# Three of eight latent token tiles through all 16384 experts at once, five by gathered expert rows

## What is computed

```python
s = jnp.einsum('thpd,hpnd->thpn', qf, sub_keys)         # 8 heads, 2 halves, 128 keys each
sv, si = lax.top_k(s, 16)
cand = sv[:, :, 0, :, None] + sv[:, :, 1, None, :]       # 256 pairs per head
top_s, pos = lax.top_k(cand, 16)                         # expert = key0 * 128 + key1
gate = softmax(top_s)
act = gelu(einsum('td,thkd->thk', x, u_tab[idx]))        # 128 experts per token
out = einsum('thk,thkd->td', gate * act, v_tab[idx])
```

## Times and profile before

| | us |
|---|---|
| median of 3 runs | 4399.74 |
| lowest and highest | 4398.01, 4403.14 |
| the profiled execution, its own time | 4396.14 |
| its span in the profile | 4394.0 |

### The profile page before, as it was taken

The page is one execution under the profiler, slowest core; times in us unless marked ns, Lnnn a source line. Parts: engine busy times, 40 slices in busy tenths (PEclk is TensorE's granted clock), DMA queues, the critical chain, the costliest instruction groups (busy, mean ns, idle before and its releaser), DMA issues.

```text
span 4394.0 us, 33588 instructions
## 1 busy us (share of the span) xinstructions
PE 3414.1 (78%) x7972; PEld 1522.3 (35%) x7972; DVE 2882.3 (66%) x6260; ACT 886.6 (20%) x2429; POOL 1509.4 (34%) x1333
## 2 busy tenths in 40 slices
PE   7875999876788876877777777787777777777777
PEld 4345444333444442332333333233333333333332
DVE  2536797657457877775775775775775774775774
ACT  1312221453412112111111111111111111111111
POOL 0100222212222223454444444444444444444343
PEclk9987999987899988899998899998988899899899
DMA  5343666666577798999999999999999999999997
GB/s 197 139 151 125 254 231 224 249 214 236 211 292 278 289 342 334 421 422 421 421 421 421 417 416 421 411 409 418 410 401 422 409 413 416 411 406 421 411 404 297
DMA packets 224511, 1494.73 MB, mean 340 GB/s; under 512 B 26264, under 2 KB 27544, under 8 KB 57550
## 3 DMA queue, kind: packets, MB, share of 16 engines
q0 software_dynamic: 186800, 1361.21, 77.1%
q1 hardware_dynamic: 36096, 126.56, 7.7%
q10 hardware_dynamic: 1440, 5.24, 0.3%
HBM read 1466.93 MB, written 26.01 MB: 340 GB/s over the span
## 4 chain that ended last, share of the span: by engine, by line
DMA 46%; PE 27%; DVE 10%; issue 9%; POOL 4%; ACT 3%; SPq 1%; POOLq 0%; DVEq 0%; ACTq 0%
DMA arena<-in_uv,idx 27%; DMA ring_e<-in_uv,idx 14%; PE wide L820 6%; PE bank L797 4%; PE bank L633 4%; PE wide L588 3%; PE bank L656 3%; PE bank L780 3%; POOL arena L547 3%; DMA arena<-in_w_q 2%; DVE ring_e L1309 2%; PE bank L601 2%; POOL ring_e L547 1%; PE bank L683 1%; ACT arena L1075 1%
## 5 line engine op out<-in xcount | busy, mean ns | idle before, releaser
L820 PE MATMUL wide<-arena 128*128 128x512 f32 x3072 | 1526.0, 655 | 496.4 <-ACT arena L1075 473.1
L1627 DVE CUSTOM_DVE_ANT_0 arena<-arena,h2e 128x1024 f32<-128x1024 f32 x768 | 926.6, 1224 | 546.3 <-DMA arena<-in_uv,idx 525.1
L547 POOL DMA_INDIRECT arena<-in_uv,idx x768 | 895.7, 1166 | 1111.7 <-PE wide L820 952.6
L820 PEld LDWEIGHTS wide<-arena 128*128 128x128 f32 x3072 | 627.5, 210 | 1392.7 <-issue 770.1
L532 POOL DMA_INDIRECT ring_e<-in_uv,idx x256 | 305.2, 1192 | 1078.4 <-PE wide L588 523.7
L820 PE MATMUL wide<-ring_e,arena 128*128 128x512 f32 x1024 | 506.0, 651 | 152.8 <-ACT arena L1075 152.7
L1075 ACT ACTIVATE arena<-ident,small 128x128 f32<-128x128 f32 x1024 | 327.5, 390 | 621.4 <-DVE small L1634 596.7
L1627 DVE CUSTOM_DVE_ANT_0 ring_e<-ring_e,h2e 128x1024 f32<-128x1024 f32 x256 | 309.0, 1224 | 176.2 <-DMA ring_e<-in_uv,idx 175.5
L1309 DVE CUSTOM_DVE_ANT_0 ring_e<-ring_e,h2e 128x1024 f32<-128x1024 f32 x256 | 307.2, 1221 | 169.1 <-DMA ring_e<-in_uv,idx 168.8
L547 POOL DMA_INDIRECT ring_e<-in_uv,idx x256 | 285.4, 1115 | 352.9 <-PE wide L820 292.4
L1072 ACT ACTIVATE small<-small 128x4 f32<-128x4 f32 x256 | 52.6, 205 | 1569.5 <-DVE small L1627 1569.5
(11 more groups left out here) (188 smaller groups left out, 2419.7 us busy)
## 6 DMA issues: line engine op xcount, KB each, us to landing
arena<-in_w_q SPq DMA_DIRECT2D x48, 512.0 KB, 9.2
ring_e<-in_w_mod POOLq DMA_DIRECT2D x8, 2048.0 KB, 8.1
arena<-in_w_cols SPq DMA_DIRECT2D x24, 512.0 KB, 3.9
arena<-in_uv,idx POOLq DMA_INDIRECT x768
arena<-in_x SPq DMA_DIRECT2D x20, 512.0 KB, 4.0
sc_d<-arena SPq DMA_DIRECT2D x36, 256.0 KB
arena<-in_w_mod SPq DMA_DIRECT2D x4, 2048.0 KB, 8.6
arena<-in_w_vg SPq DMA_DIRECT2D x16, 512.0 KB, 4.5
```

The costliest lines, as they stand in the source:

```text
L547: pool.indirect_dma_start(out=ring[k % RING], out_offset=None, in_=a["uv"], in_offset=bass.IndirectOffsetOnAxis(ap=idx[p][:, k:k + 1], axis=0)
L820: ins = pe.matmul(wide[p][:, c * 512:(c + 1) * 512], lhsT=diag[r], rhs=ring[r][:, D + c * 512:D + (c + 1) * 512], start=(first and r == 0) ...
L1627: dve.tensor_tensor_reduce(out=ring[r][:, 0:D], in0=ring[r][:, 0:D], in1=h2b[p], scale=1.0, scalar=0.0, op0=ALU.mult, op1=ALU.add, accum_o ...
```

## The change

The kernel keeps the front. Tiles 3, 4 and 5 (`C_TILES`) no longer gather. Tiles 2, 6, 7, 8, 9 (`A_TILES`) do, with a ring of 10 buffers. What follows the front is written out in two stages.

**Beats** (40). A beat has one group of four slots of tile 2 (beats 0 to 31) and a share of a choice: tile 3 in beats 0 to 9, 4 in 10 to 19, 5 in 20 to 29, 6 in 30 to 38. Behind each choice of tiles 3 to 5 come eight beats (11 to 18, 21 to 28, 31 to 38) that spread the tile's gates over all experts, four units of four tokens each: GpSimd makes for each token a 128x128 one-hot of key 0 times the gate (`ones_a`), ScalarE one of key 1 by Abs and Relu (`ones_b`), TensorE multiplies them, and ScalarE copies the 128x128 result to SBUF. For each 32 tokens SyncE stores 2 MB to DRAM (`spread_d`, 12 stores).

**Steps** (128). A step multiplies one block of 128 experts with the 384 tokens of the three tiles (8 matmuls, `scores_of`), takes Gelu (ScalarE), multiplies by the gates (`weigh`), and adds weight times `v` block to three sums (6 matmuls, `sum_rows`). Beside it goes one group of four slots of tiles 6 to 9: TensorE adds only the first half of each `v` row (`sums_half`, 4 matmuls), VectorE the other half (`halves_of`). The blocks of `u` (transposed on the host) and `v` are 512 KB each; gates come for four blocks at a time, in pieces of 512 B that lie 2 MB apart from one 32 tokens to the next. PSUM holds the sums of the three tiles.

```diff
-RING = 16
+RING = 10
+ETILES = 128
+C_TILES = (3, 4, 5)
+A_TILES = (2, 6, 7, 8, 9)
...
+UNIT = 4
+UNITS = P // UNIT
+UNITS_A_BEAT = 4
+URING = VRING = GRING = 2
+WRING = 3
+BEATS = 40
+PICK_BEATS = {3: (0, 10), 4: (10, 10), 5: (20, 10), 6: (30, 9)}
+PICK_STEPS_AT = {7: (0, 28), 8: (32, 28), 9: (64, 28)}
...
+            def store_span(t, u):
+                g = span_of(t, u)
+                sp.wait_ge(*S["g_empty"].at((t, u)))
+                src = gbuf[g % 2].rearrange("p (i t) -> p i t", t=SPAN)
+                sp.dma_start(spread_d[g], src).then_inc(*S[f"g_out{g % 2}"].mark(g, 16))
+            def load_u(i):
+                if i >= URING:
+                    sp.wait_ge(*S["s_full"].at(i - URING))
+                sp.dma_start(utb[i % URING], a["ut"][i]).then_inc(*ut_in[i % URING].mark(i, 16))
+            def load_v(i):
+                if i >= VRING:
+                    sp.wait_ge(*S["v_done"].at(i - VRING))
+                sp.dma_start(vtb[i % VRING], a["uv"][i * P:(i + 1) * P, D:2 * D]).then_inc(*vt_in[i % VRING].mark(i, 16))
+            def load_gates(gr):
+                if gr >= GRING:
+                    sp.wait_ge(*S["w_ready"].at((gr - GRING + 1) * NG - 1))
+                dst = gwb[gr % GRING].rearrange("p (g i t) -> p g i t", i=NG, t=SPAN)
+                src = spread_d[:, :, gr * NG:(gr + 1) * NG, :].rearrange("g p i t -> p g i t")
+                sp.dma_start(dst, src).then_inc(*S[f"gw_in{gr % GRING}"].mark(gr, 16))
...
+            def gather(n):
+                t, k = slot_of(n)
+                r = n % RING
+                if k == 0:
+                    pool.wait_ge(S["idx_ready"].sem, t + 1)
+                if n >= RING:
+                    pool.wait_ge(*S["a_used"].at((n - RING) // GROUP))
+                    if n - RING >= SLOTS:
+                        pool.wait_ge(*S["a_half"].at(n - RING))
...
+            def ones_for(t, u):
+                n = g_nth[t, u]
+                if n >= 2:
+                    pool.wait_ge(*S["bank_full"].at(("G", *g_tiles[n - 2])))
+                else:
+                    pool.wait_ge(*S["bank_full"].at(("hT1", NT - 1)))
+                if u == 0:
+                    pool.wait_ge(*S["sel_ready"].at(t))
+                for q in range(UNIT):
+                    k, c = u * UNIT + q, slice(q * P, (q + 1) * P)
+                    ins = pool.tensor_scalar(ones_a[n % 2][:, c], iota128[:], sel[t % 2][:, k:k + 1],
+                                             sel[t % 2][:, P + k:P + k + 1], ALU.is_equal, ALU.mult)
+                ins.then_inc(*S["ones_a"].mark((t, u)))
+            for n in range(AHEAD):
+                gather(n)
+            for b in range(BEATS):
+                for t in C_TILES:
+                    if b == choice_beat(t):
+                        for u in range(2):
+                            ones_for(t, u)
+                for t, u in units_at(b):
+                    if u + 2 < UNITS:
+                        ones_for(t, u + 2)
+                for n in range(AHEAD + b * GROUP, AHEAD + (b + 1) * GROUP):
+                    if n < SLOTS:
+                        gather(n)
...
+            def sums_half(g):
+                for n in range(g * GROUP, (g + 1) * GROUP):
+                    t, k = slot_of(n)
+                    pe.wait_ge(*S["a_diag"].at(n))
+                    if k == 0 and t != A_TILES[1]:
+                        pe.wait_ge(*S["acc_read"].at(A_TILES[A_TILES.index(t) - 1]))
+                    ins = pe.matmul(half_bank[:], lhsT=diag[n % 8], rhs=ring[n % RING][:, D:D + 512],
+                                    start=(k == 0), stop=(k == SLOTS - 1), skip_group_check=True)
+                ins.then_inc(*S["a_used"].mark(g))
...
+            def spread(t, u):
+                n = g_nth[t, u]
+                pe.wait_ge(*S["ones_a"].at((t, u)))
+                pe.wait_ge(*S["ones_b"].at((t, u)))
+                bk = bank(("G", t, u))
+                for q in range(UNIT):
+                    c = slice(q * P, (q + 1) * P)
+                    ins = pe.matmul(bk[:, c], lhsT=ones_b[n % 2][:, c], rhs=ones_a[n % 2][:, c], start=True, stop=True)
+                full(ins, ("G", t, u))
...
+            def scores_of(i):
+                pe.wait_ge(*ut_in[i % URING].at(i))
+                if i:
+                    pe.wait_ge(*S["s_empty"].at(i - 1))
+                for k in range(KD):
+                    ins = pe.matmul(s_bank[:, 0:NC], lhsT=utb[i % URING][:, k * P:(k + 1) * P],
+                                    rhs=H2T[1][:, k, P:P + NC], start=(k == 0), stop=(k == KD - 1))
+                ins.then_inc(*S["s_full"].mark(i))
+            def sum_rows(i):
+                pe.wait_ge(*vt_in[i % VRING].at(i))
+                pe.wait_ge(*S["w_ready"].at(i))
+                if i == 0:
+                    pe.wait_ge(*S["acc_read"].at(2))
+                for j in range(CN):
+                    for h, acc in enumerate(acc_c(j)):
+                        ins = pe.matmul(acc, lhsT=wtb[i % WRING][:, j * P:(j + 1) * P],
+                                        rhs=vtb[i % VRING][:, h * 512:(h + 1) * 512],
+                                        start=(i == 0), stop=(i == ETILES - 1), skip_group_check=True)
+                ins.then_inc(*S["v_done"].mark(i))
+            for i in range(ETILES):
+                scores_of(i)
+                if i:
+                    sums_half(GROUPS_A + i - 1)
+                    sum_rows(i - 1)
+            sums_half(GROUPS_A + ETILES - 1)
+            sum_rows(ETILES - 1)
...
```

ScalarE's beats (`gelu_group`, `diag_group` are the old two steps) and VectorE's beats and steps:

```diff
+                for q in range(UNIT):
+                    at = 2 * P + u * UNIT + q
+                    ins = act.activation(ones_b[n % 2][:, q * P:(q + 1) * P], iota128[:], ACT.Abs,
+                                         bias=sel[t % 2][:, at:at + 1])
...
+            for b in range(BEATS):
+                if b < GROUPS_A:
+                    gelu_group(b)
+                    diag_group(b)
...
+                for t, u in units_at(b):
+                    empty_spread(t, u)
+                    if u + 2 < UNITS:
+                        ones_for(t, u + 2)
...
+            for b in range(BEATS):
+                if b < GROUPS_A:
+                    dots_of(b)
...
+                for t, q in picks_at(PICK_BEATS, b):
+                    pick_step(t, q)
+                if b < GROUPS_A:
+                    weights_of(b)
+            for i in range(ETILES):
...
+                dots_of(GROUPS_A + i)
+                weights_of(GROUPS_A + i)
+                halves_of(GROUPS_A + i)
...
+                for t, q in picks_at(PICK_STEPS_AT, i):
+                    pick_step(t, q)
+                weigh(i)
```

More of the change, by code:

```diff
@@ L74, in stream_blocks, with picks_at, choice_beat, units_at @@
     return [(s + i, t0 + i * n, n) for i in range((t1 - t0) // n)]
+def picks_at(table, at):
+    return [(t, q) for t, (first, span) in table.items() for q in share(at - first, 0, span) if at >= first]
+def choice_beat(t):
+    return sum(PICK_BEATS[t])
+def units_at(b):
+    return [(t, u) for t in C_TILES for u in range(UNITS) if choice_beat(t) + 1 + u // UNITS_A_BEAT == b]
+def groups_now(b):
+    return b if b < GROUPS_A else None
 def build(nc, a, counts):
@@ L553, in _ @@
+            for n in range(SLOTS, SLOTS + AHEAD):
+                gather(n)
+            for i in range(ETILES):
+                for n in range(SLOTS + AHEAD + i * GROUP, SLOTS + AHEAD + (i + 1) * GROUP):
+                    if n < len(A_TILES) * SLOTS:
+                        gather(n)
         @block.tensor
@@ new lines, in _ @@
+            for b in range(BEATS):
+                if 1 <= b <= GROUPS_A:
+                    sums_full(b - 1)
+                for t in C_TILES:
+                    if b == choice_beat(t):
+                        turn_choice(t)
+                for t, u in units_at(b):
+                    spread(t, u)
+            for key in units[-4:]:
+                pe.wait_ge(*emptied(key))
+            def scores_of(i):
[6 more added lines that the diff above has]
+                ins.then_inc(*S["s_full"].mark(i))
@@ L1119, in _ @@
+            root(9)
+            for j, t in enumerate(C_TILES):
+                root(t, ybufc[j], x1c[j], 2 + j)
+            store(9)
+            for j, t in enumerate(C_TILES):
+                store(t, x1c[j])
         @block.vector
@@ new lines, in dots_of @@
+            def dots_of(g):
+                for n in range(g * GROUP, (g + 1) * GROUP):
+                    t, k = slot_of(n)
+                    r, j = n % RING, n % 8
+                    if k == 0:
+                        dve.wait_ge(*S[f"h2_in{kept(t)}"].at(t))
+                    if k % GROUP == 0 and g >= 2:
+                        dve.wait_ge(*S["a_gelu"].at(g - 2))
+                    dve.wait_ge(*landed[r].at(n))
+                    dve.tensor_tensor_reduce(out=ring[r][:, 0:D], in0=ring[r][:, 0:D], in1=h2b[kept(t)], scale=1.0,
```

(33 more changed lines are left out.)

551 lines of the change are left out of this document (337 added, 214 removed).

## The result

The changed kernel takes 4534.36 us (median of 4 runs, 4521.27 to 4545.93) against 4398.88 us for the kernel before (4 runs, 4390.67 to 4403.14): ratio 1.031, 95% interval 1.0276 to 1.0344, slower. The forecast was 4255 us in 4150 to 4410. The profiled execution took 4545.93 us with a span of 4544.0 us, so it is the slowest of the four. The changed kernel was timed in this one group of runs; where a later version is compared with it, the two times come from different groups, in which the kernel before had medians of 4398.88 to 4403.89 us.

The account below looks back on a forecast made before the run. After the front, DMA bytes were taken to bound the kernel. Front 1704, beats 780, handover 35, steps 1676, small rows 24 and tail 28 sum to 4247, given as a 4250 us span and 4255 us time, range 4150 to 4410.

Parts of the forecast that it names:

- TensorE's 6.9 us a step: Steps: TensorE's matmuls, 8 x 0.32 + 10 x 0.43, take 6.9 us, below the 13.2 us of a step.
- so DMA stays full: 127 x 13.2: Steps: the buffer ring leaves enough time, so DMA never idles and 127 steps of 13.2 us take 1676 us.
- The front and the tail: The front ends near 1704 us, 167 us more to the end of beat 10; the tail after the steps takes 28.
- A spreading beat: Beats 11 to 18 and 21 to 28: gathers wait behind GpSimd's one-hots; 28 us a beat, 448 in all.
- The one-hot at 0.4 us: Spreading beats: one GpSimd one-hot takes 0.4 us, taken from a 0.25 us select and a 0.94 us gather issue.
- the one-hots are dear: Rival, beats: at 0.94 us per one-hot, beats end 68 us later, 4320; at 1.6, 4460; chance 0.18.
- ScalarE alone sets the pace: After beat 31, in the last gate spread: 32 units at 2.6 us each on ScalarE, 83 us.
- a 512-column matmul goes every 0.43 us (16 in 7.13): Steps: TensorE's time per 512-column matmul, 0.43 us, from a row of 16 in 7.13 us.
- the rival of slow gates: Rival, steps: half-rate gate loads take 6.0 us, not 3.0, giving 4350, chance 0.12; a skill-page estimate was 4.8 a load.
- 24 us for small loads: Steps: token, score, residual and result rows, some 10 MB beside the main loads, add 24 us.
- TensorE waiting for gates rather than blocks: Sign, listed among those that would show the forecast wrong: TensorE waits for gates instead of blocks.
- TensorE at its lower clock: Rival, steps: at 1.2 GHz a step's matmuls take 13.8 us and TensorE bounds it, 4345; chance 0.08.

Follow-up runs that it names:

- e3: Changed kernel with SyncE issuing each V block load one iteration later, behind the next U block: 4371.1 us, ratio 0.9942 to the kernel before.
- e4: Changed kernel with GpSimd issuing each beat's four gathers ahead of its one-hots instead of behind them: 4401.2 us, 133 less than the changed kernel.
- e9: Both load orders exchanged (U ahead of V, gathers ahead of one-hots), half of the score matmuls left out, gates loaded through ScalarE's queue: 4227.5 us.
- both orders: Changed kernel with U loads ahead of V on SyncE and gathers ahead of one-hots on GpSimd: 4254.3 us, ratio 0.9666 to the kernel before.
- e1: Changed kernel with half of the dense score matmuls left out: 4648.5 us, 114 us more than the changed kernel.
- e7: Changed kernel with U ahead of V, gathers ahead of one-hots, and half of the score matmuls left out: 4553.9 us.

## Why the prediction was wrong, point by point

Two steps of the prediction failed in the dense steps. TensorE's 6.9 us a step was half of the true 13.75, which is worth 70 us. And "so DMA stays full: 127 x 13.2" took every load to be in time; TensorE waited for U blocks instead, which with small losses is 146 us. This second one turned the sign: 4534 less 146 is 4388, just under the time before, and with U ahead of V 4371 was measured (e3). The beats add 81 us.

- **The front and the tail** held: 174.7 against 167 us to beat 11, 28 against 28.
- **A spreading beat** was right in mechanism and near in size: 29.9 against 28 us. e4 shows that the order on GpSimd caused it, and that behind it stood GpSimd's own time.
- **The one-hot at 0.4 us** was mis-sized: 0.78, and 1.02 on average in the eight beside the choice. The nearest rows were a select, 0.25 for 128 columns, and the issue of a gather, 0.94; I chose near the lower one. The rival "the one-hots are dear" had 68 us for 0.94 each; the beats came 79 us late. "ScalarE alone sets the pace" with 2.6 us a unit failed with it: one-hots set 3.1 (44 in 34.92 us are 3.17 a unit), and ScalarE's unit itself was 2.9, as its copy, whose output is strided, took 1.03 us instead of the 0.59 of the earlier trace rows. That stretch took 137.6 us instead of 105.
- **TensorE in a step** is the first step that failed: "a 512-column matmul goes every 0.43 us (16 in 7.13)". The sixteen of that row are records of eight matmuls, since four slots with two halves each make eight, which the code says, and the forecast itself, under its low clock, speaks of "eight matmuls in 10 us". Four 512-column float32 matmuls take 3.44 us (3312.72 to 3316.16), 0.86 each, and eight of 384 columns 5.16 (3307.56 to 3312.72), 0.645 each; a step is 8 x 0.645 + 10 x 0.86 = 13.76, measured 13.75. The forecast had half of it, and so never asked what TensorE's bound would do. The Trainium skill, "FP8 and Floating Point Precision", section "TensorE Precision Notes", has true float32 as four passes through the array. An estimate by that page, with one column a cycle at 2.4 GHz, is 4 x 512 / 2400 = 0.85 us, and the trace agrees with its 0.86. Read beside the earlier trace rows it would have shown the error.
- **DMA full in the steps** is the second step that failed: share 0.94 and 363 GB/s. The bytes were right: where DMA does bound (e9), a step is 13.49 against the forecast's 13.2, at 407 instead of 421 GB/s; the gates cost 0.60 against 0.76. So the rival of slow gates did not come either: 0.60 a step is 2.4 us a load, where it had 6.0 and the estimate beside it 4.8. The pitch of 2 MB that both rest on holds in `spread_d` only between the twelve groups of 32 tokens, while the 128 rows within a group lie 128 x 32 x 4 B = 16 KB apart. On TensorE's true time alone the sum would have been 127 x 0.55 = 70 us higher, still faster than before.
- **The rest of the steps,** 15.09 - 13.75 = 1.34 us each, 170 in all, is waiting; the forecast had 24 us for small loads there, and no term for a load that is late. The forecast costed the loads as bytes and not by when each is issued: U was behind a V load that waits for a whole step, and behind the gates. "TensorE waiting for gates rather than blocks" stood among the signs of a wrong forecast; it waited for blocks, because of gates.
- **TensorE at its lower clock** did not come: 0.97 in the steps. Its 13.8 us for a step's matmuls is nearly the measured 13.75 by luck: half of the matmul time, doubled for the clock, where the time was mis-sized by two and the clock was not low.

In the sum: 81 us up to the first dense product, 70 for TensorE's time, and 146 for the waits, mostly for U, beyond the 24 us of small loads (1916 - 1700 - 70). With the order of one load exchanged the change is worth 0.6% (4371 us, ratio 0.992 to 0.9963), with both orders 3.3% (4254), with the one-hots on VectorE 6.3% (4131).

## What to carry to other kernels

Count the instructions that the code issues before dividing a group's time by the number in its row; here each float32 matmul has two records. Where a queue mixes loads, cost each load by its issue, its neighbours in the queue and its need, and not by its bytes: a load that waits for a buffer, or one of many small pieces, belongs behind the urgent ones or in another engine's queue. A rate that fits the bytes moved can be the result of the waits; change the order of two loads before believing in a bandwidth.

## What was not expected of the hardware

- Less work made it slower: half of the scores left out cost 114 us (e1) and 300 us (e7), by longer waits for loads.
- A transfer of 0.5 MB took 35.7 us with DMA at 403 GB/s, while SyncE's queue got 17.6% of the engines' time beside GpSimd's gathers.
- After a stall of 18.63 us TensorE took 5.47 us for eight records of 512 columns that take 3.60 otherwise, and the granted clock was 0.60 in the 5 us behind the stall (3103 to 3108 us of e7); so a stall costs some 2 us more than its length.
- GpSimd's one-hot of 128 columns takes 0.78 us at best and up to 3.51 beside a two-input VectorE instruction of 2.3 us; VectorE's takes 0.27.
